# Three reorderings in a hybrid streaming encoder step: constants and modulation products, second head pair, first output weight tiles

## The reference

```python
mod = silu(c) @ w_ada + b_ada                 # c: one row per group; w_ada 2048 x 6144
shift, scale, gate = split(mod, 3)
h = x * (1 + scale) + shift
qa,ka,va,ga, qb,kb,vb,gb, qi,ki,wi = split(h @ w_in)      # w_in 2048 x 5192
oa = windowed attention, 16 heads on 2 kv heads, sinks, relative bias      # group A
ob = attention over the top-k keys an indexer picks, 16 heads, bias        # group B
y  = concat(oa * silu(ga), ob * silu(gb)) @ w_out          # w_out 2048 x 2048
x  = LayerNorm(ALPHA * x + gate * y)
```

## Time and profile before

| | us |
|---|---|
| median of 3 runs | 1999.81 |
| lowest, highest | 1998.09, 2002.83 |
| profiled execution, whole time | 2001.68 |
| profiled execution, span | 2000.0 |
| mean granted clock of TensorE | 0.973 |

### The profile page before, as it was taken

One profiled execution on the slowest core, in us unless ns is written; L12 is line 12 of the kernel. 1 busy time (PEld: TensorE's weight loads), 2 busy tenths in 40 slices (PEclk: granted clock), 3 DMA queues, 4 the chain that ended last, 5 costly groups with the idle time before them and its releaser, 6 DMA issues.

```text
span 2000.0 us, 36519 instructions
## 1 busy us (share of the span) xinstructions
PE 1869.9 (93%) x13351; PEld 1561.7 (78%) x13351; DVE 979.8 (49%) x2519; ACT 626.0 (31%) x1359; POOL 680.4 (34%) x860
## 2 busy tenths in 40 slices
PE   5799999999999999999999998989999899999992
PEld 2467887679999999999999996656665688888772
DVE  2244513467777788873000004887777133342726
ACT  1122233421111111111111116988887322122120
POOL 1122211012222222222222224866666543444741
PEclk8899999979999999999999999999999999999996
DMA  7874433113222222222222244431220233346463
GB/s 226 261 250 135 124 98 111 32 38 94 85 89 85 85 86 90 85 85 85 85 85 85 85 120 115 106 84 46 58 52 19 88 121 121 122 124 182 117 216 90
DMA packets 209716, 213.27 MB, mean 107 GB/s; under 512 B 23152, under 2 KB 167280, under 8 KB 208768
## 3 DMA queue, kind: packets, MB, share of 16 engines
q1 hardware_dynamic: 178320, 172.38, 30.4%
q10 hardware_dynamic: 29952, 35.08, 5.0%
q0 software_dynamic: 1328, 4.26, 0.7%
HBM read 181.31 MB, written 34.55 MB: 108 GB/s over the span
## 4 chain that ended last, share of the span: by engine, by line
issue 45%; PE 25%; POOL 18%; ACT 5%; DVE 4%; DMA 3%; POOLq 1%; SPq 0%; ACTq 0%; DVEq 0%
POOL w_lo L1088 8%; POOL w_lo L1137 8%; PE psum L1684 4%; PE psum L1641 3%; PE psum L1663 3%; DMA ada_ring<-in_w_ada_dram 2%; PE psum L1511 2%; PE psum L1469 2%; PE psum L1512 2%; PE psum L1513 2%; ACT p_rows L972 2%; PE psum L1550 2%; PE psum L1552 1%; PE psum L1551 1%; ACT over_z_evacuated L994 1%
## 5 line engine op out<-in xcount | busy, mean ns | idle before, releaser
L1550 PE MATMUL psum<-h_hi,w_hi 128*128 128x364 f32 (+1 forms) x1728 | 577.5, 334 | 6.9 <-POOL w_lo L1088 6.2
L1552 PE MATMUL psum<-h_lo,w_hi 128*128 128x364 f32 (+1 forms) x1728 | 567.7, 329 | 0.0
L1551 PE MATMUL psum<-h_hi,w_lo 128*128 128x364 f32 (+1 forms) x1728 | 566.0, 328 | 0.0
L1088 POOL TENSOR_TENSOR w_lo<-w_raw,w_hi 128x512 fp32r<-128x512 f32 x144 | 185.5, 1289 | 701.5 <-ACT w_hi L831 701.4
L1550 PEld LDWEIGHTS psum<-h_hi,w_hi 128*128 128x128 f32 x1728 | 325.9, 189 | 44.7 <-issue 36.8
L1551 PEld LDWEIGHTS psum<-h_hi,w_lo 128*128 128x128 f32 x1728 | 325.8, 189 | 0.0
L1552 PEld LDWEIGHTS psum<-h_lo,w_hi 128*128 128x128 f32 x1728 | 325.6, 188 | 0.0
L1137 POOL TENSOR_TENSOR w_lo<-w_raw,w_hi 128x512 fp32r<-128x512 f32 x128 | 181.5, 1419 | 209.0 <-ACT w_hi L1017 209.0
L831 ACT ACTIVATE w_hi<-w_raw 128x512 fp32r<-128x512 f32 x144 | 90.7, 630 | 478.2 <-PE psum L1552 454.2
L1253 DVE MAX8 top<-scores 128x8 f32<-128x384 f32 (+6 forms) x210 | 185.4, 883 | 80.1 <-DVE scores L1256 79.9
L1733 PE MATMUL psum<-w_hi,mixed_halves 128*128 128x512 f32 x512 | 202.2, 395 | 11.1 <-POOL w_lo L1137 11.1
(11 more groups left out here) (206 smaller groups left out, 2674.2 us busy)
## 6 DMA issues: line engine op xcount, KB each, us to landing
w_raw<-in_w_in_dram SPq DMA_DIRECT2D x144, 256.0 KB, 2.8
w_raw<-in_w_out_dram SPq DMA_DIRECT2D x256, 128.0 KB, 2.9
z_transposed<-z_evacuated ACTq DMA_DIRECT2D x32, 544.0 KB, 2.7
ada_ring<-in_w_ada_dram SPq DMA_DIRECT2D x64, 256.0 KB, 3.9
ada_ring<-in_w_ada_dram SPq DMA_DIRECT2D x32, 512.0 KB, 5.1
stage<-in_w_ada_dram SPq DMA_DIRECT2D x32, 512.0 KB, 4.0
over_z_evacuated<-z_transposed SPq DMA_DIRECT2D x32, 272.0 KB, 4.5
q_transposed<-z_transposed SPq DMA_DIRECT2D x16, 272.0 KB, 4.8
```

The source lines that it names most:

```text
L1088: pool.tensor_tensor(v(wlo), raw3[ch][:, :, 0:width], v(whi).bitcast(F32), ALU.subtract).then_inc(lo_ready.sem, 1)
L1550: pe.matmul(Z, w(whi), hh[:, kt_, a:b], start=(kt_ == 0), stop=False)
L1551: pe.matmul(Z, w(wlo), hh[:, kt_, a:b], start=False, stop=False)
L1552: ins = pe.matmul(Z, w(whi), hl[:, kt_, a:b], start=False, stop=(kt_ == KT - 1))
```

## The change

Three places are changed. At the start, SyncE issues the tiles of `w_ada` first, and gives the credits after the third; ScalarE issues the seven constants itself, c first, on counts of its own (c, identity, the four others), then does silu(c) and only then the zero row. TensorE waits for the identity and silu(c), transposes c, starts the products, and does the transpose of `b_ada` and the bias lines after the product of k = 7. The load of q and tables of pair 1 moves ahead of V and G. At the end, the first two tiles of `w_out` are split in ScalarE's step NI + 1, after its copy of the last batch but one, and in GpSimd's step NI + 2, ahead of the splits of items 142 and 143. For that, the rows of the last four items are placed elsewhere: items 140 and 141 in the common columns alone, 142 and 143 in the buffer of q alone. The remaining 14 tiles of chunk 0 are written out, and the loops run over the other chunks.

```diff
+Y_STEP = NI + 1
...
-    return [(0 if i < NI - 2 else P_COLS // 2, P_COLS), (P_Q, P_END)]
+    return [(0, P_COLS), (P_Q, P_END)] if i < NI - 4 else [(0, P_COLS)] if i < NI - 2 else [(P_Q, P_END)]
...
+    loaded_c = count("loaded_c")
+    loaded_ident = count("loaded_ident")
...
     def _(sp):
-        for c in counts:
-            if c.credit:
-                sp.sem_inc(c.sem, c.credit)
-        sp.dma_start(ident[:, :], io["identity"]).then_inc(loaded_const.sem, 16)
-        sp.dma_start(c_rows[0:16, :], io["c_prompt"].rearrange("o (k p) -> (o k) p", p=P)).then_inc(loaded_const.sem, 16)
...
-            sp.wait_ge(ada_used.sem, ada_used.at(n + 1 - ADA))
+            if n >= ADA:
+                sp.wait_ge(ada_used.sem, ada_used.at(n + 1 - ADA))
...
         for i in range(ADA_SLOTS[0]):
             load_ada(0, i)
+            if i == ADA - 1:
+                for c in counts:
+                    if c.credit:
+                        sp.sem_inc(c.sem, c.credit)
...
+        load_q(1)
+        load_tab(1)
         load_v(0, 0)
         load_v(0, 1)
         load_g(0)
-        load_q(1)
-        load_tab(1)
         load_g(1)
...
     def _(act):
-        act.wait_ge(loaded_const.sem, loaded_const.at(16 * 7))
+        act.dma_start(c_rows[0:16, :], io["c_prompt"].rearrange("o (k p) -> (o k) p", p=P)).then_inc(loaded_c.sem, 16)
+        act.dma_start(c_rows[16:32, :], io["c_sample"].rearrange("o (k p) -> (o k) p", p=P)).then_inc(loaded_c.sem, 16)
+        act.dma_start(ident[:, :], io["identity"]).then_inc(loaded_ident.sem, 16)
+        act.dma_start(b_rows[:, :], io["b_ada"].rearrange("o (k p) -> (o k) p", p=P)).then_inc(loaded_const.sem, 16)
...
+        act.wait_ge(loaded_c.sem, loaded_c.at(32))
+        act.activation(c_rows[:, :], c_rows[:, :], ACT.Silu).then_inc(c_silu.sem, 1)
+        act.wait_ge(loaded_ident.sem, loaded_ident.at(16))
         act.activation(zero_row[:, :], ident[0:1, :], ACT.Copy, scale=0.0)
-        act.activation(c_rows[:, :], c_rows[:, :], ACT.Silu).then_inc(c_silu.sem, 1)
...
         for step in range(STEPS):
...
+            if step == Y_STEP:
+                for k in range(SPLIT):
+                    act.wait_ge(t_ready.sem, t_ready.at(max(BATCH_END[raw_last(RAW + k)], BATCH_END[raw_last(RAW + SPLIT + k)])))
+                    hi_out(0, 0, k)
         act.wait_ge(t_ready.sem, t_ready.at(NB))
...
-        with act.Fori(0, YN) as n:
+        for k in range(SPLIT, KT):
+            hi_out(0, 0, k)
+        with act.Fori(1, YN) as n:
...
+        def lo_out(c, k):
+            pool.wait_ge(hi_ready.sem, hi_ready.at(c * KT + (k + (NM - NF) * WCH + 1)))
+            pool.tensor_tensor(wlo[:, k % SPLIT, :], raw[:, k % RAW, :], whi[:, k % SPLIT, :].bitcast(F32), ALU.subtract).then_inc(lo_ready.sem, 1)
...
+            if step == Y_STEP + 1:
+                for k in range(SPLIT):
+                    lo_out(0, k)
+        for k in range(SPLIT, KT):
+            lo_out(0, k)
+        with pool.Fori(1, YN * len(Y_GROUPS)) as c:
...
     def _(dve):
...
+        dve.wait_ge(loaded_const.sem, loaded_const.at(16 * 4))
...
     def _(pe):
-        pe.wait_ge(loaded_const.sem, loaded_const.at(16 * 7))
+        pe.wait_ge(loaded_ident.sem, loaded_ident.at(16))
         pe.wait_ge(c_silu.sem, c_silu.at(1))
...
-        pe.wait_ge(lines_ready.sem, lines_ready.at(1))
-        pe.wait_ge(small_c.sem, small_c.at(2))
+        def lines_and_bias():
...
         for k in range(KT):
             ada_step(0, k)
+            if k == 7:
+                lines_and_bias()
+        pe.wait_ge(lines_ready.sem, lines_ready.at(1))
+        pe.wait_ge(small_c.sem, small_c.at(2))
         columns(0)
```

More of the change, by code:

```diff
@@ L998, in copy_T @@
             ins.then_inc(pt_ready.sem, 1)
[L1000 to L1007, removed]
         def hi_out(g, n, k):
@@ L1017, in hi_out @@
             act.activation(whi[:, k % SPLIT, :], raw[:, k % RAW, :], ACT.Copy).then_inc(hi_ready.sem, 1)
+        for step in range(STEPS):
+            due = batches_due(step)
+            for j in range(max(2, len(due))):
+                if j < len(due):
+                    copy_T(due[j])
+                if j < 2 and 1 <= step <= NI:
+                    exp(step - 1, j)
+            if step == Y_STEP:
+                for k in range(SPLIT):
+                    act.wait_ge(t_ready.sem, t_ready.at(max(BATCH_END[raw_last(RAW + k)], BATCH_END[raw_last(RAW + SPLIT + k)])))
+                    hi_out(0, 0, k)
+        act.wait_ge(t_ready.sem, t_ready.at(NB))
         def std(g):
@@ L1133, in _ @@
                     mix_halves(i)
-        with pool.Fori(0, YN * len(Y_GROUPS)) as c:
+            if step == Y_STEP + 1:
[4 more added lines that the diff above has]
+        with pool.Fori(1, YN * len(Y_GROUPS)) as c:
             for k in range(KT):
-                pool.wait_ge(hi_ready.sem, hi_ready.at(c * KT + (k + (NM - NF) * WCH + 1)))
-                pool.tensor_tensor(wlo[:, k % SPLIT, :], raw[:, k % RAW, :], whi[:, k % SPLIT, :].bitcast(F32), ALU.subtract).then_inc(lo_ready.sem, 1)
+                lo_out(c, k)
     @block.vector
@@ L1447, in _ @@
     def _(pe):
-        pe.wait_ge(loaded_const.sem, loaded_const.at(16 * 7))
+        pe.wait_ge(loaded_ident.sem, loaded_ident.at(16))
         pe.wait_ge(c_silu.sem, c_silu.at(1))
         pe.transpose(bank(0)[:, 0:32], c_rows[:, :], ident[0:32, 0:32]).then_inc(small_T.sem, 1)
-        pe.transpose(bank(1)[:, 0:48], b_rows[:, :], ident[0:48, 0:48]).then_inc(small_T.sem, 1)
-        for gi in range(2):
-            ins = pe.matmul(bank(2 + gi)[0:16, 0:NREL], relb[:, 16 * gi:16 * gi + 16], onehot[:, :], start=True, stop=True)
-        ins.then_inc(small_T.sem, 1)
+        cTv = cT[:, :].rearrange("p (w k) -> p k w", w=2)
         pe.wait_ge(small_c.sem, small_c.at(1))
-        cTv = cT[:, :].rearrange("p (w k) -> p k w", w=2)
-        pe.wait_ge(lines_ready.sem, lines_ready.at(1))
-        pe.wait_ge(small_c.sem, small_c.at(2))
+        def lines_and_bias():
+            pe.wait_ge(loaded_const.sem, loaded_const.at(16 * 4))
+            pe.transpose(bank(1)[:, 0:48], b_rows[:, :], ident[0:48, 0:48]).then_inc(small_T.sem, 1)
+            for gi in range(2):
+                ins = pe.matmul(bank(2 + gi)[0:16, 0:NREL], relb[:, 16 * gi:16 * gi + 16], onehot[:, :], start=True, stop=True)
+            ins.then_inc(small_T.sem, 1)
         def ada_step(p, k):
```

8 lines of the change are left out of this document (3 added, 5 removed).

## The result

The changed kernel took 1980.81 us (median of 4 executions, 1977.74 to 1986.62), the kernel before 1998.95 in the same comparison (4 executions, 1995.09 to 2002.83). The ratio is 0.9911, 95% interval 0.9893 to 0.993: 17.8 us won, with 14 to 21 in the interval. The forecast was 1986.6, and its range ended at 1981.5, just above the measured median. So the direction was right, and the gain lies outside the range.

What follows compares the result with a forecast made beforehand. TensorE, busy for 93% of the span, was taken as the bound, with at most some 130 us of idleness to win. Terms 7.3 + 1.8 + 4.1 = 13.2 us, off the median 1999.81, gave 1986.6 us; range 1981.5 to 1994.

Steps and rivals of the forecast that it cites:

- rival C: Second head pair: the whole stall goes, 6.3 us there; sum 17.7 us, time 1982.1; chance 0.12.
- the clock's term of part 3: Output projection's start: idleness of 1.8 us is too short for the clock to fall, winning 2.66 us.
- part 3: Output projection's start: two w_out tiles split early win 1.45 us of wait plus 2.66 of clock, 4.1 us, bounds 0 and 4.1.
- part 1: Kernel start: tiles asked for first, constants on ScalarE, bias lines behind k = 7; 7.3 us won, bounds 2.0 and 8.4.
- part 2: Second head pair: q and tables loaded ahead of V and G win 1.8 us, bounds -1.0 and 6.3.
- A start made earlier by t brings the whole stage forward by about t: First stage, to 170 us: freed slots trigger tile loads, so an earlier first product carries through; 7.8 us gain.
- The identity was set at 5.8: Kernel start: the identity's load lands at 5.8 us and does not decide the first product, set at 7.0.
- 0.5 us net for the lines behind k = 7: First stage: 2.73 us of bias lines in a 2.0 us average gap cost 0.5 us, bounds 0 and 2.7.
- to about 1228: Second head pair: V is asked for at 1221.6, so `p_v` waits for it to about 1228, some 3 us.
- the exponential gains 1.4 us where 0.5 was set: Second head pair: G lands at 1231, so item 9's first exponential begins at 1233.1, not 1233.60: 0.5 us won.
- The second term, 1.3 us of ScalarE's wait for transposes: Second head pair: TensorE has done the transposes by then, so ScalarE's 1.30 us wait for them goes.
- Rival B: Clock falls anyway at the output projection and G lands at 1232.5: sum 9.05 us, time 1990.8; chance 0.15.

Runs made afterwards that it cites:

- e0: The kernel before once more, no edit, as a control: 2000.64 us, ratio 0.9995 to the kernel before.
- e1: The kernel before with only the new start (loads, silu and bias lines as in the changed kernel): 1989.47 us, ratio 0.9946.
- e13: The kernel before with only the new start, run again: 1992.27 us, ratio 0.9959.
- e2: The kernel before with only q and tables of pair 1 loaded ahead of V and G: 1996.99 us, ratio 0.9984.
- e3: The kernel before with only the early split of two w_out tiles and its row placement: 1994.04 us, ratio 0.9965.
- e5: The changed kernel with the bias lines and their waits ahead of the first w_ada product again: 1995.52 us, ratio 0.9979.
- e8: The kernel before with only the b_ada transpose and bias lines moved behind k = 7, loads in old order: 1994.15 us, ratio 0.9966.
- e9: The kernel before with extra unread products filling gaps in the second half of the last indexer logits: 1996.92 us, ratio 0.9984.
- e10: The changed kernel with V and G loaded ahead of q and tables again, as before: 1988.70 us, ratio 0.9949.
- e4: The changed kernel again, no edit: 1987.54 us, ratio 0.9952 to the kernel before.
- e12: The changed kernel a third time, no edit: 1983.88 us, ratio 0.9931 to the kernel before.
- e6: The changed kernel with extra unread products filling gaps in the second half of the last indexer logits: 1984.65 us, ratio 0.9931.
- e7: The changed kernel with eight extra products in the wait ahead of the first output projection product: 1985.06 us, ratio 0.9945.
- e11: The changed kernel with extra products both in the last logits and ahead of the output projection: 1983.02 us, ratio 0.9912.
- e14: The changed kernel with both fillings (last logits, ahead of output projection), run again beside the changed kernel: 1983.38 us, ratio 0.9923.

## Why the prediction was right or wrong

**In short.** The three places gave 12.2 us against the 13.2 forecast, so the sum itself was nearly right. The step that failed is the reading that the change wins only in the three places it touches, with everything else fixed: the low clock in the rest of the span stood in the sum and in the range at nothing. In the pair of profiles the projection, which no part touches, was 6.1 us shorter, and over the executions of the first comparison the clock accounts for some 5.6 us of the gain. The median lies only 0.7 us below the range, and 0.9 us of that way is the kernel before, which came out at 1998.95 beside it and not at the 1999.81 that the forecast was taken from. But a gain of 17.8 us needed rival C's whole stall, which did not go. Beside this, the clock's term of part 3, 2.66 us, was too large.

The stages of the profiles tell more than the totals, since the clock's falls lie in known places. All in us, without the last 37 us or so, behind the last product with `w_out`: the first product of the projection (the start's stage); from there to the first `q_k`; from the first to the last `q_k`; from the last `q_k` to the last product with `w_out`.

| kernel | start | projection | scores | rest |
|---|---|---|---|---|
| before | 248.0 | 968.4 | 342.9 | 403.8 |
| e0 before | 250.6 | 968.7 | 343.4 | 403.1 |
| e1 part 1 | 241.5 | 967.1 | 342.4 | 403.9 |
| e13 part 1 | 240.8 | 963.9 | 342.5 | 406.2 |
| e2 part 2 | 249.7 | 961.2 | 340.6 | 402.1 |
| e3 part 3 | 246.7 | 967.0 | 342.9 | 401.4 |
| e5 lines ahead | 249.3 | 967.2 | 341.7 | 401.0 |
| e8 lines behind | 244.4 | 968.6 | 343.9 | 402.4 |
| e9 before, filled | 250.7 | 962.1 | 344.0 | 403.0 |
| e10 parts 1, 3 | 241.7 | 961.7 | 343.7 | 399.8 |
| changed | 241.8 | 962.3 | 342.2 | 401.8 |
| e4 changed | 243.2 | 963.7 | 342.2 | 402.8 |
| e12 changed | 240.3 | 961.6 | 341.6 | 400.9 |
| e6 filled logits | 242.8 | 962.4 | 341.0 | 399.6 |
| e7 filled output | 239.8 | 962.4 | 340.3 | 399.0 |
| e11 both | 243.6 | 962.3 | 339.8 | 400.2 |
| e14 both | 240.0 | 963.7 | 340.6 | 399.4 |

**Part 1: right, 7.6 us against 7.3.** Ten profiles with the new start begin the projection at 241.5 on average, five with the old one at 249.1. "A start made earlier by t brings the whole stage forward by about t" held in e5 and e8 too. Two smaller steps were off. The identity was set at 5.8 and said not to decide; it landed at 6.8, and decided. The 0.5 us net for the lines behind k = 7 was too much, for they lie within the waits for tiles. The prediction did not say which of the two moves wins: e5 and e8 show that moving the lines wins 4.4 us by itself, and the order of the loads the other 3, but only once the lines are moved. Of the rule in the Trainium skill (ScalarE: Activation LUTs, What ACT_TABLE_LOAD costs), the trace agrees on the load and again not on the drain: silu starts 1.29 us after its table load began.

**Part 2: right, 2.1 us against 1.8.** Nine profiles with q ahead take 341.1 from the first to the last `q_k`, eight without 343.2. A single pair can show less: in the first one it was 0.7. The mechanism is the one described: V and G are late in place of q, `p_v` waits 2.79 us where "to about 1228" meant some 3, and the exponential gains 1.4 us where 0.5 was set, since G landed a microsecond earlier. The second term, 1.3 us of ScalarE's wait for transposes, was too large: 0.63 us of it stays. Its reason, that TensorE would have done the transposes by then, did not hold: TensorE came out of the wait for V at half clock again, and was through with them only at 1221.3.

**Part 3: the mechanism right, the second term too large.** The idle time shrinks by 1.45 us as worked out, to 10.6 to 10.8 between the last `q_k` and the first product with `w_out` in every profile with it. What failed is "if the clock stays, 2.66 us are won", counted in full for the reason that 1.8 us of idleness is less than 2.9. In seven unfilled profiles with the early split the clock fell after 2.1 us of idleness in five (e3, e4, e5, e12, changed) and stayed in two (e6, e10). The stage takes 403.5 without part 3 (seven profiles), 401.0 with it (seven), and 399.5 where the wait is filled (three). So the part is worth 2.5 us on average against 4.1. Of this 1.45 is the wait, and some 1.1 the clock in place of 2.66. Where the clock stays without filling (e6, e10) the stage takes 399.7, and the 4.1 nearly hold. The 2.66 were also read from a long fall: by windows of half a microsecond the low clock there lasts 6.8 us in before, e1 and e13 (stage 404.6) and 3.4 in e0, e2, e8 and e9 (402.7). Rival B had this half right, but not its G at 1232.5.

**The sum** by stages is 7.6 + 2.1 + 2.5 = 12.2 us, against 13.2 forecast. No rival's mechanism came about as a whole; that the first comparison gave C's 17.7 is luck.

**What was left out is the size of chance, and where it lies.** The projection takes 967.8 us on average in the six profiles in which the clock fell early in the last logits, 962.4 in the seven in which it fell late, 962.6 in the four in which the gaps were filled. That is 5.4 us in a stretch that no part touches. The profile of before showed it, with two windows at 0.50 in a row, and the prediction did not look: it read its three places and took the rest as fixed, though its own profiled execution had a mean clock of 0.973, where 100 executions of this kernel average 0.9787.

**The totals agree.** A straight line through all 226 executions with a recorded clock, each kernel with a level of its own, says this: 0.001 more mean granted clock goes with 0.92 us less (within 0.11). The four executions of the changed kernel in the first comparison had a mean clock of 0.9848, the kernel before 0.9787 over its 100 (of the four beside them only the profiled one has its clock on record): 0.0061, or 5.6 us of the 18. What is left, some 12.5, is near the sum of the stages. By this line the parts alone win, at equal clock, 7.4, 2.5 and 4.2 us (each within 1.2 to 1.8), which sums to more than the whole's 11.4, but not by more than these bounds.

The three comparisons of the same two kernels gave 17.8, 9.6 and 13.8 us; the changed kernel's 20 executions average 1986.0 (1987.1 without the first four), and the 100 of the kernel before 1999.9, a gain of 13.9 (12.8). The forecast of 1986.6 is close to this mean, which is partly luck, since its clock terms were too large and what the clock gave elsewhere was left out. Its range was built from the bounds of the terms, with nothing for the median of a few executions of a kernel that scatters by 3.7 us (standard deviation) and by 5.4 in one stretch.

**Still open** is whether the early fall near 400 us is chance alone. It was seen in five of the six profiles without filled logits whose first product came at 10 us or later, and in one of the seven where it came near 7. By the mean clocks the start alone raises it by 0.0012 only (19 executions, within 0.0012), the whole change by 0.0027 (20 executions, within 0.0014), some 2.5 us. So the changed kernel's higher clock is more than scatter, but where in the span it comes from is open. It may be that an earlier start makes the early fall rarer; the runs don't settle it, and no mechanism for it was shown.

## What to carry to other kernels

Ask of a start what its first product really waits for: here small products of no hurry, which needed the last of seven loads, held up a stage that runs at the pace of its ring, and each microsecond of an earlier start came back whole. Read the granted clock along the whole span before you forecast, also where the change is not; a stretch of short products with gaps in which it sits at half is a term that comes and goes, and belongs in the range. When a wait is cut so that the clock "should" stay, count the clock's part at half, until a profile has shown it more than once.

## What the runs showed that was not expected

- The clock fell with TensorE at work, a microsecond behind the end of a wait of 2.09 us, and in other executions of nearly the same program it did not. In the logits of the kernel before it fell behind ten microseconds in which TensorE was busy for 8.21, with gaps of some 0.26 us. The Trainium skill (TensorE: Matmul & The Clock Gate, A second HAM failure mode: psum-queue depth-cycling) tells of such micro-idles between groups of products that let the gate oscillate. The runs agree: in e9, with the gaps filled, the clock stayed at 1.00 through the stretch.
- The same page of the Trainium skill (What's actually happening) calls the number of slow products at the start of a kernel run-variable, and puts the price of this ramp under 1% of a typical span. The stretch near 400 us is not at the start; by these runs it varies too, by 5.4 us of 2000, 0.27%, which is more than parts 2 and 3 of this change win by their stages.
- Extra products that compute nothing made the kernel before 3.2 us faster (e9; by its interval 0.4 to 6.2).
- The load of the identity (64 KB) landed in 1.9 us ahead of the first tiles and in 4.9 us beside them; the sinks, 8 KB, took 2.9 and 5.8 us.
